# Low parts of the gate/up weight pairs made by ScalarE and an accumulating transfer instead of VectorE

## The chip, the core and the metric

The kernel runs on one core of a Trainium2 chip. The core has five engines that run side by side and meet only at semaphores: TensorE (PE, matrix products), VectorE (DVE), ScalarE (ACT), GpSimd (POOL) and SyncE (SP, which here only issues transfers). DMA engines move data between the chip's large memory (HBM) and the core's on-chip memory (SBUF). The metric is the device time of one execution in microseconds; lower is better.

## What is computed

A two-layer decoder trunk on 512 tokens of width 1024 in float32. Each layer has a mixer (pooling and gating in layer 0, dilated attention and retention in layer 1), an attention into 256 memory tokens, and a SwiGLU feed-forward part, each with its own norm and residual. The change touches the feed-forward part only:

```
D_FF = 2816
def swiglu(h, w_gate_up, w_down):
    gu = h @ w_gate_up
    g, u = gu[..., :D_FF], gu[..., D_FF:]
    return (jax.nn.silu(g) * u) @ w_down
...
h = h + swiglu(rmsnorm(h, ffn_norm[layer]), ffn_w_gate_up[layer], ffn_w_down[layer])
```

## The kernel before

**Three products for one.** Each float32 operand is split into a high part, the value rounded to TensorE's fast format fp32r, and a low part, the rest. A product is then hi x hi + hi x lo + lo x hi, three matmuls that add up in one PSUM bank. For the weights, ACT writes the high part (`w_hi` from `raw`, a copy that rounds) and DVE the low part (`w_lo = raw - w_hi`).

**Units and the ring.** Weights come from HBM in units of 128 x 1024 (512 KB). `raw`, `w_hi` and `w_lo` are rings of four units (RING = 4). SP loads them in order: before it loads a unit into a slot of `raw` it waits until the low part of the slot's last unit is made (semaphore `lo_ready`, which counts units). ACT may write `w_hi` in a slot when TensorE is done with what stood there.

**Gate/up in pairs.** The feed-forward part has 22 column tiles for gate and as many for up. The first four of each (PLAIN = 4) go through an ordinary loop. The other 18 steps of two tiles (PAIRS = 18, numbered q = 0 to 17, two units each, so that a pair fills half a ring) are computed with seven block products in the place of eight (a Strassen-like scheme). Products 1, 2, 4 and 7 read the weight pair's own parts (`w_hi`, `w_lo`), and products 5, 6 and 3 read sums of its blocks, which DVE makes into `s_f` (`first_sums`, `last_sum`) and ACT and DVE split into `s_hi` and `s_lo` (`sum_hi`, `sum_lo`). A product is 4 x 3 matmuls of 128 x 256.

**The order on TensorE** is `pair_steps()`: product 1 and 7 of pair q, product 3 of pair q-1, then products 6, 2, 4 and 5 of pair q, then product 1 of pair q+1, and so on. Product 1 of a pair is the first to read its `w_lo`, and the one that waits for it (`pe.wait_ge(lo_ready, pair_unit(layer, q) + 2)`).

**The order on ACT**, each q of the pair loop in `ffn`: copy product 6 of q out of PSUM (`copy_product`), `sum_hi(q+1)`, for even q two gate steps, `copy_product(q+1, 1)`, `pair_hi(q+2)` (the high parts of pair q+2, 128 x 2048), `copy_product(q+1, 7)`. TensorE's product 4 of pair q+1 waits for that last copy.

**The order on DVE**, each q: `last_sum(q+1)`, `pair_lo(q+1)` (the low parts of pair q+1), the quarters 11 and 21 of pair q, `sum_lo(q+1)`, quarter 22, `first_sums(q+2)`. `first_sums` of a pair overwrites one block of `raw` with a sum (semaphore `s3_ready`), and `pair_hi` waits for that.

POOL adds squares for the norms elsewhere. In the pair loop it has nothing to do, and it issues no transfer anywhere.

Of the kernel before, what the change touches and what calls it, by code (L numbers as in the profile page):

```python
# [35 lines left out]
F32 = mybir.dt.float32  # L36
F32R = mybir.dt.float32r
ACT = mybir.ActivationFunctionType
ALU = mybir.AluOpType
# [25 lines left out]
PAIRS = FT - PLAIN  # L65
# [11 lines left out]
F_DN, F_END = 2 * FT, 2 * FT + 2 * len(DOWN)  # L77
# [98 lines left out]
def program(nc, d):  # L176
    who, aux_at = aux_plan()

    with ExitStack() as ctx:
        def sem(name):  # L180
            return ctx.enter_context(nc.semaphore(name))
# [77 lines left out]
        raw = fixed("raw", [P, RING, UW])  # L259
        w_hi = fixed("w_hi", [P, RING, UW], F32R)  # L260
        w_lo = fixed("w_lo", [P, RING, UW], F32R)
# [88 lines left out]
        bhi_ready = sem("bhi_ready")  # L350
        blo_ready = sem("blo_ready")
        s3_ready = sem("s3_ready")
        s_ready = sem("s_ready")
        shi_ready = sem("shi_ready")
        slo_ready = sem("slo_ready")
# [118 lines left out]
        def pair_unit(layer, q):  # L474
            return F_UNIT[layer] + 2 * PLAIN + 2 * q

        def pair_cols(ring, layer, q):

            n = pair_unit(layer, q) % RING
            return ring[:, n:n + 2, :]  # L480

        def region_a(q):
            return accs[2 * (q % 2)][:, 0:S // 2]
# [170 lines left out]
        def _(act):  # L654
# [186 lines left out]
            def ffn(layer):  # L841
# [22 lines left out]
                def pair_hi(q):  # L864

                    n = pair_unit(layer, q)
                    act.wait_ge(raw_in[n % RING], 16 * (n // RING + 1))
                    act.wait_ge(s3_ready, PAIRS * layer + q + 1)
                    slot_free(act, n - RING)
                    slot_free(act, n + 1 - RING)  # L870
                    act.activation(pair_cols(w_hi, layer, q), pair_cols(raw, layer, q), ACT.Copy).then_inc(hi_ready, 2)  # L871

                def sum_hi(q):

# [332 lines left out]
        @block.gpsimd  # L1207
        def _(pool):
            pool.memset(warm_w[:, :], 0.0).then_inc(const_set, 1)
            pool.memset(mean_w[:, :], 1.0 / D).then_inc(const_set, 1)  # L1210
            pool.memset(mexp[:, :], -0.5).then_inc(const_set, 1)
            pool.memset(a_pad[:, :, 0:PAD], 0.0).then_inc(const_set, 1)
            pool.wait_ge(const_set, 4)

            def power(dst, src, n):
                pool.tensor_tensor(dst, src, mexp[:, 0:n], ALU.pow).then_inc(rstd_ready, 1)

            def norm_power(norm):

                pool.wait_ge(aux_free_v, freed_v(aux_at["mean", norm]))  # L1220
                power(rstd_tok[:, :], var_e[:, :], TT)

            def add_squares(norm, tiles=KT):
                for j in range(1, tiles):
                    n = (KT - 1) * (norm - 1) + j
                    pool.wait_ge(sq_ready, 8 * (norm - 1) + j + 1)
                    if j > 1:
                        pool.wait_ge(sq_added, n - 1)
                    pool.tensor_tensor(sqsum[:, :], sqsum[:, :], tmp[:, j % 2, :], ALU.add).then_inc(sq_added, 1)  # L1229

            pool.wait_ge(var_ready, 1)
            power(rstd_m[:, :], var_m[:, :], MT)
            pool.wait_ge(var_ready, 2)
            power(rstd_tok[:, :], var_e[:, :], TT)
            pool.wait_ge(c0_in, 16 * 5)

            pool.affine_select(out=ws_t[:, :, :], in_=ws_t[:, :, :], compare_op=ALU.is_ge, fill=0.0, base=0,
                               pattern=[[0, 4], [1, P]], channel_multiplier=-1).then_inc(ws_masked, 1)

            steps = 0  # L1240
            for g, win in enumerate(WINDOWS):
                pool.wait_ge(acc_drained, MIX_ACC[0] + A_A + g + 1)
                if g == 0:
                    pool.wait_ge(var_ready, 3)
                    power(rstd_v[:, :], var_v[:, :], TT)
                if g:

                    pool.wait_ge(win_ready, g)
                src, width = a_pad[:, g, :], 1
                buf = 0  # L1250
                while width < win:
                    last = 2 * width == win
                    if last and g >= 1:

                        pool.wait_ge(d_ready, g)
                    dst = wsum[:, 2 if last else buf, :]
                    lo = 2 * width - 1
                    ins = pool.tensor_tensor(dst[:, lo:PAD + S], src[:, lo:PAD + S],
                                             src[:, lo - width:PAD + S - width], ALU.add)
                    if last:  # L1260
                        ins.then_inc(win_ready, 1)
                    else:
                        ins.then_inc(win_step, 1)
                        steps += 1
                        pool.wait_ge(win_step, steps)
                    src, buf, width = dst, 1 - buf, 2 * width
            for layer in range(LAYERS):
                if layer:
                    add_squares(3)
                    norm_power(3)  # L1270

                    for r in range(16):
                        dst = rot_tile(r)
                        pool.wait_ge(rot_half, r + 1)
                        pool.tensor_tensor(dst, dst, tmp[:, 2 + r % 2, :], ALU.add).then_inc(rot_ready, 1)
                    for h in range(RET_H):
                        pool.wait_ge(rvar_ready, h + 1)
                        pool.tensor_tensor(rrstd[:, h, :], rvar[:, h, :], mexp[:, :], ALU.pow)\
                            .then_inc(rrstd_ready, 1)
                for norm in (3 * layer + 1, 3 * layer + 2):  # L1280
                    add_squares(norm)
                    norm_power(norm)
            add_squares(6, KT - 2)
            for e in range(2):
                pool.wait_ge(aux_free_v, freed_v(aux_at["mean", 6, e]))
                power(rstd_tok[:, 2 * e:2 * e + 2], var_e[:, 2 * e:2 * e + 2], 2)
# [3 lines left out]
        def _(dve):  # L1290
# [8 lines left out]
            def split(n, i=None):  # L1299
                if n >= UNITS:  # L1300
                    return
                s = n % RING
                dve.wait_ge(hi_ready, lin(n + 1, i, RING))
                dve.tensor_tensor(w_lo[:, s, :], raw[:, s, :], w_hi[:, s, :].bitcast(F32), ALU.subtract)\  # L1304
                    .then_inc(lo_ready, 1)
# [322 lines left out]
            def ffn(layer):  # L1628
# [50 lines left out]
                def last_sum(q, i):  # L1679

                    n, sums = pair_unit(layer, q), s_f[q % 2]
                    if q >= 2:
                        dve.wait_ge(product_done, product_at(layer, q - 2, 3))
                    dve.wait_ge(dve_step, i)
                    dve.tensor_tensor(sums[:, 2, :], sums[:, 1, :], raw[:, n % RING, 512:1024], ALU.add).then_inc(s_ready, 1)

                def pair_lo(q):
                    dve.wait_ge(hi_ready, pair_unit(layer, q) + 2)
                    dve.tensor_tensor(pair_cols(w_lo, layer, q), pair_cols(raw, layer, q),  # L1689
                                      pair_cols(w_hi, layer, q).bitcast(F32), ALU.subtract).then_inc(lo_ready, 2)  # L1690
# [181 lines left out]
                for q in range(PAIRS):  # L1872
                    last = q == PAIRS - 1
                    if q and q % 2 == 0:
                        up_second(q - 1)
                    if last:
                        split(u0 + F_DN)
                        split(u0 + F_DN + 1)
                    else:
                        if q:  # L1880
                            last_sum(q + 1, i)
                        pair_lo(q + 1)
                    if q == 0:
                        b_lo_part(3)
                    if last:
                        quarter(q, 11)
                        quarter(q, 22)
                        act_lo_part(7)
                        quarter(q, 21)
                    else:  # L1890
                        quarter(q, 11)
                        quarter(q, 21)
                        sum_lo(q + 1)
                        quarter(q, 22)
                    if q + 2 < PAIRS:
                        i = first_sums(q + 2)
                    if q % 2:
                        up_first(q)
                        up_tile(q)
                    if q in (10, 12, 14):  # L1900
                        act_lo_part(4 + (q - 10) // 2)
                    if last:
                        act_lo_part(8)
# [1008 lines left out]
```

## Time and profile before

| | us |
|---|---|
| median of 3 runs (1385.01 to 1385.16) | 1385.08 |
| span of the profiled execution | 1383.4 |
| TensorE busy (99% of the span) | 1374.1 |
| VectorE busy (70%) | 961.5 |
| ScalarE busy (48%) | 663.8 |
| GpSimd busy (8%) | 114.9 |

The span runs from the first to the last instruction of one profiled execution on the core; the median of the times lies 1.7 us above it. Busy time of an engine counts its computing instructions; registers, semaphores and issued transfers are not counted. A wait is put down to the engine and line that ended it.

### The profile page before, as it was taken

What the parts mean: (1) busy time and instruction counts of PE and PEld (TensorE: products, weight loads), DVE (VectorE), ACT (ScalarE), POOL (GpSimd) and SP (SyncE); (2) the same over time, 40 slices, a digit from 0 to 9 for tenths busy, and PEclk for the clock granted to TensorE, in tenths of its full rate; (3) what the DMA queues carried; (4) which work ended last, traced back from release to release, by engine and by line L of the source; (5) the groups of instructions that cost most, each with busy time, mean ns of one, the idle gap of its engine ahead of it and who ended that gap; (6) DMA issues with size and microseconds to landing.
All of it is one profiled execution on the core that took longest, in us unless ns stands there. A gap on an engine that the chain in (4) does not pass through costs nothing.

```text
span 1383.4 us, 21582 instructions
## 1 busy us (share of the span) xinstructions
PE 1374.1 (99%) x8404; PEld 1225.5 (89%) x8404; DVE 961.5 (70%) x1335; ACT 663.8 (48%) x984; POOL 114.9 (8%) x89
## 2 busy tenths in 40 slices
PE   9999999999999999999999999999999999999997
PEld 8988888889999998998887788988888999998897
DVE  6656556469878877774578755765549888888674
ACT  6633534355455553352756634543454545545341
POOL 0012200110000000110211211100020000000011
PEclk9999999999999999999999999999999999999999
DMA  9721320222323233325321212542132223233321
GB/s 345 268 91 61 107 92 31 91 92 77 122 92 122 93 107 107 120 95 167 97 87 46 82 41 77 185 150 77 46 107 79 105 98 116 93 122 98 116 92 62
DMA packets 42285, 147.22 MB, mean 106 GB/s; under 512 B 5072, under 2 KB 5584, under 8 KB 42192
## 3 DMA queue, kind: packets, MB, share of 16 engines
q1 hardware_dynamic: 38592, 136.79, 28.8%
q10 hardware_dynamic: 3600, 9.12, 1.9%
q8 instruction: 67, 1.10, 0.3%
q14 instruction: 26, 0.21, 0.1%
HBM read 143.80 MB, written 2.10 MB: 105 GB/s over the span
## 4 chain that ended last, share of the span: by engine, by line
PE 96%; DVE 2%; issue 1%; ACT 1%; DMA 0%; POOLq 0%; POOL 0%; ACTq 0%; DVEq 0%
PE acc L2173 17%; PE acc L2175 17%; PE acc L2174 17%; PE acc L2521 8%; PE acc L2522 7%; PE acc L2523 7%; PE acc L2221 3%; PE acc L2223 3%; PE acc L2222 3%; PE aux L2572 2%; PE aux L2571 2%; PE aux L2570 2%; PE aux L2523 1%; PE aux L2522 1%; PE aux L2521 1%
## 5 line engine op out<-in xcount | busy, mean ns | idle before, releaser
L1304 DVE TENSOR_TENSOR w_lo<-raw,w_hi 128x1024 fp32r<-128x1024 f32 x165 | 205.6, 1251 | 123.6 <-ACT w_hi L663 123.2
L663 ACT ACTIVATE w_hi<-raw 128x1024 fp32r<-128x1024 f32 x165 | 173.2, 1052 | 98.6 <-PE acc L2175 55.2
L1229 POOL TENSOR_TENSOR sqsum<-sqsum,tmp 128x512 f32<-128x512 f32 x40 | 60.0, 1501 | 960.3 <-ACT tmp L950 637.0
L2173 PE MATMUL acc<-u_hi,w_hi 128*128 128x512 f32 x352 | 138.7, 394 | 0.0
L2175 PE MATMUL acc<-u_hi,w_lo 128*128 128x512 f32 x352 | 137.2, 390 | 0.0
L2174 PE MATMUL acc<-u_lo,w_hi 128*128 128x512 f32 x352 | 137.1, 389 | 0.0
L2521 PE MATMUL acc<-b_hi,s_hi 128*128 128x256 f32 x432 | 122.4, 283 | 0.0
L2522 PE MATMUL acc<-b_lo,w_hi 128*128 128x256 f32 x432 | 122.3, 283 | 0.0
L2522 PE MATMUL acc<-b_lo,s_hi 128*128 128x256 f32 x432 | 122.2, 283 | 0.0
L2523 PE MATMUL acc<-b_hi,w_lo 128*128 128x256 f32 x432 | 122.2, 283 | 0.0
L2523 PE MATMUL acc<-b_hi,s_lo 128*128 128x256 f32 x432 | 122.2, 283 | 0.0
L2521 PE MATMUL acc<-b_hi,w_hi 128*128 128x256 f32 x432 | 122.2, 283 | 0.0
L2173 PE MATMUL acc<-y_hi,w_hi 128*128 128x512 f32 x256 | 100.1, 391 | 0.0
L2175 PE MATMUL acc<-y_hi,w_lo 128*128 128x512 f32 x256 | 99.7, 389 | 0.0
L2174 PE MATMUL acc<-y_lo,w_hi 128*128 128x512 f32 x256 | 99.6, 389 | 0.0
L2173 PE MATMUL acc<-act_hi,w_hi 128*128 128x512 f32 (+1 forms) x252 | 92.6, 367 | 0.0
L2174 PE MATMUL acc<-act_lo,w_hi 128*128 128x512 f32 (+1 forms) x252 | 92.2, 366 | 0.0
L2175 PE MATMUL acc<-act_hi,w_lo 128*128 128x512 f32 (+1 forms) x252 | 92.1, 365 | 0.0
L884 ACT ACTIVATE tmp<-acc 128x256 f32<-128x256 f32 x108 | 40.5, 375 | 96.4 <-PE acc L2523 96.4
L1689 DVE TENSOR_TENSOR w_lo<-raw,w_hi 128x2048 fp32r<-128x2048 f32 x36 | 82.2, 2284 | 2.2 <-ACT w_hi L871 2.2
L2521 PEld LDWEIGHTS acc<-b_hi,s_hi 128*128 128x128 f32 x432 | 82.9, 192 | 0.2
L2521 PEld LDWEIGHTS acc<-b_hi,w_hi 128*128 128x128 f32 x432 | 82.9, 192 | 0.1
(311 smaller groups left out, 3611.0 us busy)
## 6 DMA issues: line engine op xcount, KB each, us to landing
raw<-in_weights SPq DMA_DIRECT2D x253, 512.0 KB, 3.4
hT<-in_x_t ACTq DMA_DIRECT2D x4, 512.0 KB, 8.2
x_tok<-in_x ACTq DMA_DIRECT2D x4, 512.0 KB, 5.1
raw<-in_weights SPq DMA_DIRECT2D x5, 256.0 KB, 6.1
mem_tok<-in_mem ACTq DMA_DIRECT2D x2, 512.0 KB, 5.8
out_h<-out_f SPq DMA_DIRECT2D x2, 512.0 KB, 2.6
memT<-in_mem_t SPq DMA_DIRECT2D x3, 256.0 KB, 6.3
cs_d<-in_cs_d ACTq DMA_DIRECT2D x1, 512.0 KB, 4.3
```

What stands on the lines that cost most here:

```text
L663: act.activation(w_hi[:, s, :], raw[:, s, :], ACT.Copy).then_inc(hi_ready, 1)
L1229: pool.tensor_tensor(sqsum[:, :], sqsum[:, :], tmp[:, j % 2, :], ALU.add).then_inc(sq_added, 1)
L1304: dve.tensor_tensor(w_lo[:, s, :], raw[:, s, :], w_hi[:, s, :].bitcast(F32), ALU.subtract)\
L1689: dve.tensor_tensor(pair_cols(w_lo, layer, q), pair_cols(raw, layer, q), pair_cols(w_hi, layer, q).bitcast(F32), ALU.subtract).then_inc(lo ...
L2173: pe.matmul(out, w_h, x_h, start=first, stop=False)
L2174: pe.matmul(out, w_h, x_l, start=False, stop=False)
L2175: return pe.matmul(out, w_l, x_h, start=False, stop=last)
L2221: pe.matmul(out, x_h[:, k, tok], w_hi[:, s, w], start=(k == 0), stop=False)
L2222: pe.matmul(out, x_h[:, k, tok], w_lo[:, s, w], start=False, stop=False)
L2521: pe.matmul(out, hi[:, w], x_h, start=(k == 0 and m in (1, 2, 7)), stop=False, skip_group_check=True)
L2522: pe.matmul(out, hi[:, w], x_l, start=False, stop=False, skip_group_check=True)
L2523: ins = pe.matmul(out, lo[:, w], x_h, start=False, stop=(k == 3), skip_group_check=True)
```

## The change

For pairs q = 2 to 17 of both layers (32 pairs), DVE no longer makes the low parts. Instead

- ACT, right behind the high parts, writes `-round(raw)` into `w_lo` (a copy of 128 x 2048 with scale -1, counted by `neg_ready`);
- POOL waits for that and issues a transfer of `raw` into `w_lo` that adds (`accum_op=ALU.add`), 128 x 2048, 1 MB, SBUF to SBUF, so that `w_lo` holds `raw - w_hi`;
- POOL then waits for the earlier low parts (`lo_ready`), for the pair's last sum (`s_ready`, which also reads `raw`) and for the transfer (`low_in`), and adds 2 to `lo_ready`, on which both TensorE and SP wait.

Pairs 0 and 1 keep `pair_lo`. Of the last iteration, DVE waits until the last pair's count is in before it adds its own.

```
+        def nth(layer, q):
+            return (PAIRS // 2 - 1) * layer + q // 2
...
                     act.activation(pair_cols(w_hi, layer, q), pair_cols(raw, layer, q), ACT.Copy).then_inc(hi_ready, 2)
+                    if q >= 2:
+                        act.activation(pair_cols(w_lo, layer, q), pair_cols(raw, layer, q), ACT.Copy, scale=-1.0)\
+                            .then_inc(neg_ready, 1)
...
+            def low_parts(layer, q):
+                n = pair_unit(layer, q)
+                pool.wait_ge(neg_ready, (PAIRS - 2) * layer + q - 1)
+                pool.dma_start(pair_cols(w_lo, layer, q).bitcast(F32), pair_cols(raw, layer, q), accum_op=ALU.add)\
+                    .then_inc(low_in[q % 2], 16)
+                pool.wait_ge(lo_ready, n)
+                pool.wait_ge(s_ready, PAIRS * layer + q + 1)
+                pool.wait_ge(low_in[q % 2], 16 * nth(layer, q))
+                pool.sem_inc(lo_ready, 2)
...
                 for norm in (3 * layer + 1, 3 * layer + 2):
                     add_squares(norm)
                     norm_power(norm)
+                for q in range(2, PAIRS):
+                    low_parts(layer, q)
...
                     if last:
+                        dve.wait_ge(lo_ready, u0 + F_DN)
                         split(u0 + F_DN)
                         split(u0 + F_DN + 1)
+                    elif q:
+                        last_sum(q + 1, i)
                     else:
-                        if q:
-                            last_sum(q + 1, i)
-                        pair_lo(q + 1)
+                        pair_lo(1)
```

On ACT, in the pair loop of layer 0, the rows from the first copy ahead of `pair_hi(2)` to `sum_hi(3)` before:

```order
L884 ACTIVATE tmp<-acc 128x256
L871 ACTIVATE w_hi<-raw 128x2048
L884 ACTIVATE tmp<-acc 128x256
L896 ACTIVATE tmp<-acc 128x256
L884 ACTIVATE tmp<-acc 128x256
L876 ACTIVATE s_hi_64<-s_f_60 128x1536
```

and now:

```order
L893 ACTIVATE tmp<-acc 128x256
L877 ACTIVATE w_hi<-raw 128x2048
L879 ACTIVATE w_lo<-raw 128x2048
L893 ACTIVATE tmp<-acc 128x256
L905 ACTIVATE tmp<-acc 128x256
L893 ACTIVATE tmp<-acc 128x256
L885 ACTIVATE s_hi_64<-s_f_60 128x1536
```

The negated write stands behind the high parts and ahead of the copy of product 7, of a gate step and of the next sum's high parts.

On DVE, one iteration of the pair loop in layer 0, from `last_sum(3)` on, before:

```order
L1685 TENSOR_TENSOR s_f_61<-s_f_61,raw 128x512
L1689 TENSOR_TENSOR w_lo<-raw,w_hi 128x2048
L1709 TENSOR_TENSOR tmp<-aux,tmp 128x256
L1709 TENSOR_TENSOR tmp<-acc,tmp 128x256
L1694 TENSOR_TENSOR s_lo_63<-s_f_61,s_hi_65 128x1536
```

and now:

```order
L1707 TENSOR_TENSOR s_f_61<-s_f_61,raw 128x512
L1731 TENSOR_TENSOR tmp<-aux,tmp 128x256
L1731 TENSOR_TENSOR tmp<-acc,tmp 128x256
L1716 TENSOR_TENSOR s_lo_63<-s_f_61,s_hi_65 128x1536
```

The 128 x 2048 subtraction is gone; nothing else changes its place.

On POOL, from layer 0's last norm ahead of its feed-forward part to the norm behind it, now (before, the row with DMA is not there):

```order
L1225 TENSOR_TENSOR rstd_tok<-var_e,mexp 128x4
L1244 DMA w_lo<-raw 128x2048 x16
L1238 TENSOR_TENSOR sqsum<-sqsum,tmp 128x512 x7
```

The 16 transfers stand between the two norms, on a queue that held no transfer.

## Rows read from the trace of the kernel before

**Rows 1.** Page, busy time of each engine (share of the span) xinstructions.

```profile
PE 1374.1 (99%) x8404; PEld 1225.5 (89%) x8404; DVE 961.5 (70%) x1335; ACT 663.8 (48%) x984; POOL 114.9 (8%) x89
```

**Rows 2.** Page, shares of the chain that ended last, by engine.

```profile
PE 96%; DVE 2%; issue 1%; ACT 1%; DMA 0%; POOLq 0%; POOL 0%; ACTq 0%; DVEq 0%
```

**Rows 3.** Stretches of both pair loops: busy us of each engine, clock, DMA.

```profile
core 0: us, PE busy (x) PEld busy (x) DVE busy (x) ACT busy (x) POOL busy (x), PEclk, DMA share, GB/s
325.00:495.00 170.00, 170.00 (x1404) 169.34 (x1403) 143.97 (x183) 85.68 (x113) 0.00 (x0) 1.00 0.30 106
1080.00:1250.00 170.00, 170.00 (x1418) 169.90 (x1418) 139.78 (x180) 87.10 (x117) 0.00 (x0) 1.00 0.30 109
```

**Rows 4.** Timeline of PE at first matmuls of products: start us, us, what.

```profile
407.53 0.28 PE L2521 MATMUL acc<-b_hi,w_hi 128*128 128x256 f32 x1
407.65 0.28 PE L2522 MATMUL acc<-b_lo,w_hi 128*128 128x256 f32 x1
...
414.73 0.28 PE L2521 MATMUL acc<-b_hi,w_hi 128*128 128x256 f32 x1
...
417.61 0.28 PE L2521 MATMUL acc<-b_hi,w_hi 128*128 128x256 f32 x1
```

**Rows 5.** Timeline of ACT in the same pair: start us, us, what, idle before.

```profile
409.17 0.38 ACT L884 ACTIVATE tmp<-acc 128x256 f32<-128x256 f32 x1 [4.00 <-PE acc L2523]
410.07 1.91 ACT L871 ACTIVATE w_hi<-raw 128x2048 fp32r<-128x2048 f32 x1 [0.52 <-DVE raw L1674]
411.89 0.37 ACT L884 ACTIVATE tmp<-acc 128x256 f32<-128x256 f32 x1
413.49 0.38 ACT L884 ACTIVATE tmp<-acc 128x256 f32<-128x256 f32 x1 [1.23 <-PE acc L2523]
413.77 1.48 ACT L876 ACTIVATE s_hi<-s_f 128x1536 fp32r<-128x1536 f32 x1
```

**Rows 6.** Timeline of DVE in the same pair.

```profile
412.83 0.68 DVE L1685 TENSOR_TENSOR s_f<-s_f,raw 128x512 f32<-128x512 f32 x1
413.43 2.29 DVE L1689 TENSOR_TENSOR w_lo<-raw,w_hi 128x2048 fp32r<-128x2048 f32 x1
```

**Rows 7.** Groups by line and form: xcount, busy us, mean ns, idle before.

```profile
L1689 DVE TENSOR_TENSOR w_lo<-raw,w_hi 128x2048 fp32r<-128x2048 f32 x36 | 82.2, 2284 | 2.2 <-ACT w_hi L871 2.2
L871 ACT ACTIVATE w_hi<-raw 128x2048 fp32r<-128x2048 f32 x36 | 69.0, 1916 | 15.3 <-DVE raw L1674 8.3 <-issue 6.7
```

**Rows 8.** Timeline of SP's queue: the two loads (1 MB) of one pair issued.

```profile
405.04 0.92 SPq L638 DMA_DIRECT2D raw<-in_weights  x2
```

**Rows 9.** Transfers from 404.5 to 410.5: GB/s in 40 slices of 0.15 us, queue.

```profile
GB/s 0 0 0 0 0 0 0 0 0 0 273 137 27 82 246 328 410 410 382 437 437 410 410 410 437 437 410 437 437 246 164 27 0 0 0 0 0 0 0 0
q1 hardware_dynamic: 288, 1.05, 50.7%
raw<-in_weights SPq DMA_DIRECT2D x2, 512.0 KB, 3.7
```

**Rows 10.** Timeline in layer 0: ACT's high parts of pair 2, PE's product 1 of pair 2.

```profile
340.99 1.92 ACT L871 ACTIVATE w_hi<-raw 128x2048 fp32r<-128x2048 f32 x1 [0.42 <-issue]
...
347.05 0.28 PE L2521 MATMUL acc<-b_hi,w_hi 128*128 128x256 f32 x1
```

**Rows 11.** The same high parts of pair 2 in layer 1, on ACT.

```profile
1085.31 1.92 ACT L871 ACTIVATE w_hi<-raw 128x2048 fp32r<-128x2048 f32 x1 [0.42 <-issue]
```

**Rows 12.** A group of POOL instructions by line and form, columns as in rows 7.

```profile
L1229 POOL TENSOR_TENSOR sqsum<-sqsum,tmp 128x512 f32<-128x512 f32 x40 | 60.0, 1501 | 960.3 <-ACT tmp L950 637.0 <-ACT tmp L672 322.7
```

**Rows 13.** Stretches at the program's end, columns as in rows 3.

```profile
1368.00:1372.00 4.00, 4.00 (x36) 4.00 (x35) 2.65 (x7) 0.42 (x1) 0.00 (x0) 1.00 0.02 6
1372.00:1376.00 4.00, 3.36 (x29) 3.15 (x28) 1.33 (x4) 0.08 (x1) 0.00 (x0) 1.00 0.65 262
1376.00:1383.00 7.00, 1.01 (x6) 0.71 (x6) 1.42 (x4) 1.89 (x3) 0.70 (x1) 0.68 0.40 150
```

More of the change, by code:

```diff
@@ L352, in program @@
         s3_ready = sem("s3_ready")
+        neg_ready = sem("neg_ready")
+        low_in = [sem(f"low_in{e}") for e in range(2)]
         s_ready = sem("s_ready")
```

## The prediction

> **What bounds the kernel.** I read the busy shares first: TensorE has 99% of the span, VectorE 70%, ScalarE 48% [rows 1]. The chain that ended last agrees: 96% of it is TensorE [rows 2]. Then I looked at the two stretches that the change touches. In both pair loops TensorE is busy for all of 170 us at full clock [rows 3]. So it waits for nobody there, and work taken from DVE gives no time back by itself. What can change the time is a wait of TensorE that is not there now. The only thing of this change that TensorE reads is a pair's low part, at the start of product 1. The question is whether the new way delivers it in time.
>
> **The clock of a pair.** Call t(q) the start of product 1 of pair q. In one pair of the steady state it is 407.53, and the next pair's is 417.61 [rows 4]: 10.08 us, seven products of 12 matmuls at 0.12 us, 1.44 us each. Before, the low parts that are needed at 417.61 come from DVE's subtraction at 413.43, 2.29 us long, so at 415.72 [rows 6]: 1.9 us of slack.
>
> **What goes.** 32 subtractions of 2284 ns [rows 7], 73 us of DVE. They lay beside TensorE's work with 1.9 us of slack, so their going is worth nothing. DVE's other work in the loop waits for products.
>
> **What comes on ACT.** 32 negated writes of 128 x 2048. The trace has no such write with a scale, but the same shape and copy takes 1916 ns [rows 7], and behind one the next instruction starts 1.82 us after it began (410.07 to 411.89) [rows 5]. In all 61 us on an engine busy for about half of the stretch. Queued behind it is the copy of product 7, for which product 4 waits. It would start at 411.89 + 1.92 = 413.81 and end at 414.18, and product 4 starts at 414.73 [rows 4, 5]. That just holds, so the delayed copies cost nothing; the next sum's high parts come at most about 1 us later, and the product that reads them is seven microseconds off.
>
> **What comes on the path.** The low parts are now ready after high parts, negated write, and transfer. Let D be the time from the end of the negated write to TensorE's release: POOL wakes, writes the transfer's descriptors, the data move, the semaphore comes back, POOL adds to `lo_ready`. Without any wait, the high parts start 2.54 us after t [rows 4, 5], so there are 10.08 - 2.54 - 1.82 - 1.92 = 3.8 us for D.
>
> Once TensorE waits, a tighter loop closes. On ACT `pair_hi(q+2)` is queued behind the copy of product 1 of pair q+1, which itself needs t(q+1). That copy starts 409.17 - 407.53 = 1.64 us after t [rows 4, 5]; an instruction behind such a copy starts 0.28 us later (413.49 to 413.77) [rows 5]; the high parts take 1.82 and the negated write 1.92. So t(q+2) = t(q+1) + 5.66 + D, against 10.08 now. The wait is D - 4.42 **for each pair**, and the next pair cannot start its chain earlier while TensorE stands. It is not shared between two pairs, although the ring has room for two.
>
> **The size of D.** No row shows an accumulating transfer, nor one issued by POOL. The nearest is a plain 1 MB: the two loads of a pair. They are issued from 405.04, for 0.92 us [rows 8], so the second near 405.5, and each lands 3.7 us after its issue, 409.2 in all. The bytes have stopped there too [rows 9]. That is 4.2 us. The 16 DMA engines were busy for 50.7% of 6 us [rows 9], 3.0 us for one MB. To add, a DMA engine has to read the old `w_lo` as well as `raw`, twice the bytes read, so I take another 3.0. For the three semaphore hops and POOL's own writing of descriptors I take 0.8: more than the 0.46 that SP takes for each of its two issues [rows 8], less than the 1.5 us of a small POOL instruction [rows 12]. D = 4.2 + 3.0 + 0.8 = 8.0 us.
>
> Its bounds: 4.5 if the second read is free, which needs reads to be no limit at all; 6.0 if it is half hidden; 11.7 if the two reads and the write go one after another and POOL needs 1.5 (4.2 + 3.0 + 3.0 + 1.5). A gain is excluded, since TensorE waits nowhere in the stretch. Twice the bytes to read is the nearest, as the plain loads already run at 410 to 437 GB/s [rows 9], a level that looks like a ceiling.
>
> By the Trainium skill (DMA: Bandwidth & Descriptors, section on the anatomy of one DMA on the gpsimd path) such a transfer costs about 2.0 us fixed and its bytes at 436 GB/s, 4.4 us for 1 MB; the trace's 4.2 agrees. Its page Collectives: The Full Stack (section on the bandwidth ceiling) says that an adding transfer is not slowed by the add but by its two source reads, and runs at half the rate of a copy. By these two pages D would be 2.0 + 2 x 2.4 = 6.8 us, an estimate, and the change would cost 80 us instead of what follows. No row here shows either of them for an adding transfer.
>
> **The sum.** In each layer pairs 3 to 17 wait D - 4.42 = 3.58 us, 15 x 3.58 = 53.7. Pair 2 has a chain of its own: its high parts start at 340.99, behind ACT's gate step, the negated write would end at 344.73, and product 1 starts at 347.05 [rows 10]. Its wait is D - 2.32 = 5.68. Layer 1 has the same place at 1085.31 [rows 11]. So (53.7 + 5.7) x 2 = 118.8 us, or 32 D - 137 in general. Span 1383.4 + 118.8 = 1502.2, and 1.7 us lie around the span: **1504 us**.
>
> **Costed at nothing.** SP now issues the loads of pair q+2 near t(q), 2 us later than before. They land after 4.2 us, and their first sum is needed 10 us after t(q). The adding transfer starts 5.7 us after t, when the load is through, so the two do not share DMA engines. If that cover fails, a transfer gains up to 3.0 us. DVE's wait for `lo_ready` in the last iteration ends before t(17), ahead of what it computes there. POOL's next norm comes long after its last transfer.
>
> **The rivals.**
> *No wait, no change* (4%): D is 3.8 or less, and 1385 stands. It needs a 1 MB adding transfer faster than the plain one's 4.2. TensorE's saturation holds in this case too, so faster is no more than 1%: it would need a wait that DVE ends, and the pair loops have none.
> *Cheap second read* (14%): reads and adds overlap and D lies between 4.5 and 6.2. At 5.5 the sum gives 32 x 5.5 - 137 = 39, 1424 us. For it: both sides are SBUF and HBM is not involved. Against it: the same DMA engines, already full with one read.
> *The clock falls too* (16%): TensorE would stand 3.6 us in every 13.7. The trace shows full clock while it is busy for 3.36 of 4 us, and a mean of 0.68, so partly its lower level of 1.2 GHz, when it was busy for 1.0 of 7 us [rows 13]. The new loop lies between. At half clock the one product between t and ACT's copy takes 1.44 us longer, and only that one stands on the loop: 32 x 1.44 = 46, so 1550 us. The skill (TensorE: Matmul & The Clock Gate, section on oscillation) tells of a kernel whose waits put the clock down again in every tile. That would be this case.
> *A slow maker of descriptors or a slow adder* (15%): POOL makes 128 rows of descriptors with reads and writes, and a POOL add of only 128 x 512 already takes 1.5 us [rows 12]. At D = 12 the sum is 247, 1632 us; from D = 11 on this case holds.
> *Forecast* (50%): D from 6.2 to 11, 1446 to 1600 us, likeliest 1504.
>
> **How the numbers follow.** A measurement of this kernel can tell about 0.2%, 2.8 us, from no change; that needs D below 4.4. Slower has 95%, same 4%, faster 1%. The range runs from 1430 (D = 5.7) to 1620 (D = 11.6); it leaves out no change, half of the cheap read and two thirds of the slow adder, some 2 in 10.
>
> **What would show it.** Right: TensorE's matmul at product 1 waits about 3.6 us once in every pair from 2 to 17, 32 times, longer at pair 2, and nowhere else new. A pair's period is 13.7. ACT shows a second 1.9 us instruction behind each `w_hi`, then 8 us to the next product 1. DVE busy falls by 73 us, ACT rises by 61. If waits stand at every second pair only, the loop over the copy is wrong and the one over `first_sums` holds. If periods are right but D is 6 or 12, only its size was wrong. If the copy of product 7 makes product 4 wait, the slack of 0.5 us was misread. A PEclk below 1.00 in the pair loops is the clock rival.

## The result and the profile after

The changed kernel takes 1519.9 us (median of 4 runs, 1516.9 to 1523.6) against 1385.1 us: the ratio is 1.097, with a 95% interval of 1.096 to 1.099. Forecast were 1504 us and a range of 1430 to 1620. The span of the profiled execution grew from 1383.4 to 1516.8 us, by 133.4.

The page of the kernel after: first the busy time of each engine, then two rows of forty slices of the span (busy tenths of TensorE, and its granted clock), then the adding transfers as a queue (packets, MB, share of 16 engines) and as a group of issues (KB, us from issue to landing).

```profile
PE 1416.4 (93%) x8404; PEld 1261.1 (83%) x8404; DVE 893.0 (59%) x1303; ACT 719.8 (47%) x1016; POOL 143.0 (9%) x121
...
PE   9999999997778879999999999999998878879998
...
PEclk9999999998898999999999999999999999999999
...
q0 software_dynamic: 4608, 33.56, 11.0%
...
w_lo<-raw POOLq DMA_DIRECT2D x32, 1024.0 KB, 7.0
```

Against [rows 1], TensorE issues the same 8404 matmuls but is busy for only 93% of a longer span. The missing time sits in two places of the forty slices, the two pair loops. The clock's digit falls below nine in the first of them; in the second the mean is 0.93, as a row further down shows. The groups by instruction name the work: DVE loses the 32 subtractions of 2284 ns [rows 7], 73 us, and ACT gets 32 writes of 1902 ns, 61 us. (The busy figures of the whole engine move by 68.5 and 56.0 only, because neighbouring records overlap by some 0.1 us and the page counts that time once.)

TensorE's waits, the two rows on the pair loops (us in all, times, longest; the other six, elsewhere, are of 1.2 us or less, once each):

```profile
PE acc L2544 <- POOLq L1249: 89.2, 32, 4.7
PE acc L2544 <- ACT tmp L893: 1.4, 2, 0.7
```

L2544 is the first matmul form of products 1, 7, 4 (L2521 in [rows 4]) and L1249 is POOL's `sem_inc(lo_ready, 2)`. So TensorE now waits for the low parts once in each of the 32 pairs, a wait that did not exist before, and twice for a copy of ACT, in all 1.4 us. One turn of the loop, on ACT, POOL and TensorE (start us, us, what, and in brackets the idle time before it and what ended it):

```profile
411.88 0.58 PE L2544 MATMUL acc<-b_hi,w_hi 128*128 128x256 f32 x1 [3.64 <-POOLq L1249]
...
426.33 0.38 PE L2544 MATMUL acc<-b_hi,w_hi 128*128 128x256 f32 x1 [2.79 <-POOLq L1249]
...
439.49 0.58 PE L2544 MATMUL acc<-b_hi,w_hi 128*128 128x256 f32 x1 [2.83 <-POOLq L1249]
```

```profile
414.85 0.39 ACT L893 ACTIVATE tmp<-acc 128x256 f32<-128x256 f32 x1 [9.13 <-PE acc L2546]
415.13 1.90 ACT L877 ACTIVATE w_hi<-raw 128x2048 fp32r<-128x2048 f32 x1
416.93 1.90 ACT L879 ACTIVATE w_lo<-raw 128x2048 fp32r<-128x2048 f32 x1
418.73 0.38 ACT L893 ACTIVATE tmp<-acc 128x256 f32<-128x256 f32 x1
```

```profile
402.53 0.88 POOL L1244 DMA_DIRECT2D w_lo<-raw  x1 [13.47 <-ACT w_lo L879]
...
419.20 0.87 POOL L1244 DMA_DIRECT2D w_lo<-raw  x1 [15.80 <-DVE s_f L1707]
```

Read it as a circle. Product 1 starts at 411.88; ACT can copy it at 414.85, and that copy holds up the next pair's high parts (415.13) and negated write (416.93, through at 418.83). POOL issues the transfer at 419.20, and TensorE gets product 1 of the next pair at 426.33, 7.5 us after the negated write's end. From 426.33 to 439.49 are 13.16 us, where [rows 4] show 10.08.

Three stretches and the granted clock in them: inside the wait that ends at 411.88, just behind it, and each pair loop as a whole.

```profile
core 0: us, PE busy (x) PEld busy (x) DVE busy (x) ACT busy (x) POOL busy (x), PEclk, DMA share, GB/s
408.00:411.00 3.00, 0.24 (x3) 0.04 (x1) 3.00 (x6) 0.00 (x0) 0.00 (x0) 1.00 0.25 49
412.00:415.00 3.00, 3.00 (x15) 3.00 (x16) 0.01 (x1) 0.15 (x1) 0.00 (x0) 0.51 0.66 232
325.00:535.00 210.00, 172.20 (x1258) 168.68 (x1257) 98.36 (x151) 101.58 (x115) 12.47 (x14) 0.90 0.54 143
1130.00:1340.00 210.00, 174.83 (x1279) 169.35 (x1278) 108.70 (x160) 105.70 (x118) 11.34 (x13) 0.93 0.54 143
```

After a wait of 3.64 us the clock is at 0.51, the 1.2 GHz level, and 3 us hold 15 matmuls where [rows 4] have one each 0.12 us, 25. This is why ACT's copy above comes 2.97 us behind t, not 1.64.

### The profile page after: what moved, and what is told of

It is laid out like the page before. It is cut to its first block and busy times, and to the rows that moved or that the text cites. A ratio compares the mean times of both kernels' runs of the same rounds, so it can differ in the third digit from the quotient of the medians.

```text
span 1516.8 us, 21648 instructions
## 1 busy us (share of the span) xinstructions
PE 1416.4 (93%) x8404; PEld 1261.1 (83%) x8404; DVE 893.0 (59%) x1303; ACT 719.8 (47%) x1016; POOL 143.0 (9%) x121
## 5 line engine op out<-in xcount | busy, mean ns | idle before, releaser
L2544 PE MATMUL acc<-b_hi,w_hi 128*128 128x256 f32 x432 | 141.1, 327 | 90.6 <-POOLq L1249 89.2
L2544 PEld LDWEIGHTS acc<-b_hi,w_hi 128*128 128x128 f32 x432 | 97.5, 226 | 97.6 <-POOLq L1249 95.7
L2545 PE MATMUL acc<-b_lo,w_hi 128*128 128x256 f32 x432 | 136.7, 317 | 0.0
L2546 PE MATMUL acc<-b_hi,w_lo 128*128 128x256 f32 x432 | 136.5, 316 | 0.0
L2544 PE MATMUL acc<-b_hi,s_hi 128*128 128x256 f32 x432 | 123.8, 287 | 0.0
L2545 PEld LDWEIGHTS acc<-b_lo,w_hi 128*128 128x128 f32 x432 | 98.1, 227 | 0.1
L2546 PEld LDWEIGHTS acc<-b_hi,w_lo 128*128 128x128 f32 x432 | 98.0, 227 | 0.0
```

The costliest lines, as they stand in the source:

```text
L2544: pe.matmul(out, hi[:, w], x_h, start=(k == 0 and m in (1, 2, 7)), stop=False, skip_group_check=True)
L2545: pe.matmul(out, hi[:, w], x_l, start=False, stop=False, skip_group_check=True)
L2546: ins = pe.matmul(out, lo[:, w], x_h, start=False, stop=(k == 3), skip_group_check=True)
```

## The experiments

All times are medians; each kernel is compared with the kernel before in the same series. "After" is the changed kernel. The kernel before took 1385.2 us in each series of experiments; after was timed in the series of the result, against 1385.1 us. D is, as in the prediction, the time from the end of the negated write to TensorE's product 1.

**1. The negated writes alone.** POOL's transfers go, DVE subtracts as before, behind the negated write (the subtraction overwrites it).

```
-                for q in range(2, PAIRS):
-                    low_parts(layer, q)
...
-                    elif q:
-                        last_sum(q + 1, i)
                     else:
-                        pair_lo(1)
+                        if q:
+                            last_sum(q + 1, i)
+                            dve.wait_ge(neg_ready, (PAIRS - 2) * layer + q)
+                        pair_lo(q + 1)
```

> ACT's negated write stays where it is, but POOL issues no transfer: DVE waits for the negated write and makes the low parts itself by its subtraction, as before. Computes the same as before. Theory (the transfer's time is the whole cost, ACT's extra 1.9 us hides): negated write ends 6.3 us after t(q), subtraction 2.3 us more, 8.7 of 10.08, so no wait of TensorE at product 1: 1385 to 1387 us. Rival (ACT's queue is the cost: the copies of products 7 and 6 behind the negated write make TensorE wait): 0.5 us or more at product 4 in most pairs, 1400 us and above.

Measured: 1388.8 us, ratio 1.0026 (1.0015 to 1.0037). So ACT's 61 us of extra work cost 3.6 us, small but not nothing: above the 1385 to 1387 of the theory, far below the 1400 of the rival. Where: TensorE's wait at product 4 of pair 1, once in each layer, and ACT, then PE, in a pair of the steady state.

```profile
PE acc L2542 <- ACT tmp L893: 1.4, 2, 0.7
...
346.88 0.39 PE L2542 MATMUL acc<-b_hi,w_hi 128*128 128x256 f32 x1 [0.70 <-ACT tmp L893]
```

```profile
405.39 1.90 ACT L879 ACTIVATE w_lo<-raw 128x2048 fp32r<-128x2048 f32 x1
407.19 0.36 ACT L893 ACTIVATE tmp<-acc 128x256 f32<-128x256 f32 x1
...
407.66 0.34 PE L2542 MATMUL acc<-b_hi,w_hi 128*128 128x256 f32 x1
```

The copy of product 7 runs from 407.19 to 407.55 and product 4 starts at 407.66, 0.11 us behind. The slack of 0.55 us that the prediction read is used up: periods are 10.11 to 10.13 us here (one is 10.41) and 10.08 before. Pair 1 takes 11.19, 0.96 us more, in each layer. From product 1 of pair 0 to that of pair 17 the two loops are 1.9 and 1.6 us longer than before, together 3.5. The rest of the 133 us must come from the transfer and what its waits bring about.

**2. A plain transfer.** The same 1 MB from `raw` to `w_lo`, without the add; the low parts are then the raw weights, so the result is wrong.

```
-                pool.dma_start(pair_cols(w_lo, layer, q).bitcast(F32), pair_cols(raw, layer, q), accum_op=ALU.add)\
+                pool.dma_start(pair_cols(w_lo, layer, q).bitcast(F32), pair_cols(raw, layer, q))\
```

> The transfer that POOL issues copies raw into w_lo in the place of adding it (the low parts of pairs 2 to 17 are wrong: they hold the raw weights). Same bytes written, half the bytes read. Theory (the second read is what makes the data phase twice as long): bytes move in 2.6 us in the place of 4.9, D falls from 7.45 to about 5.1, 32 x 5.1 - 137 = 26 us over before, about 1411 us, clock mostly full. Rival (what POOL's queue and descriptor writing cost dominates, whatever is moved): D stays at 7 or more, 1490 to 1520 us.

Measured: 1415.8 us, ratio 1.0217 (1.0200 to 1.0234). Without the add 104 of the 135 us are gone. TensorE's wait, the transfer's median landing time, and the transfer's queue in a window of 10 us around one of them:

```profile
PE acc L2544 <- POOLq L1249: 18.5, 31, 1.8
...
w_lo<-raw POOLq DMA_DIRECT2D x32, 1024.0 KB, 4.6
...
q0 software_dynamic: 144, 1.05, 27.3%
```

D is 4.9 to 5.1 us in most pairs, which is the sum of what the prediction made of the plain parts: 4.2 for 1 MB and 0.8 for the hops. At 5.0 the sum 32 D - 137 gives 23 us of the 30.7 measured. The trace accounts for the rest: some pairs have a D of 5.2 to 5.8, so with each pair's own D the sum is 26; TensorE waits for the copy of product 7 at pair 1 (1.9), and the negated write ends later behind t than 5.66 (3.4 in all). That makes 31.5, where the span grew by 30.0.

**3. An adding transfer of half the size.** Only the pair's first unit (512 KB) is added; the second unit keeps the negated high parts, so half of each pair's low parts are wrong.

```
-                pool.dma_start(pair_cols(w_lo, layer, q).bitcast(F32), pair_cols(raw, layer, q), accum_op=ALU.add)\
+                pool.dma_start(w_lo[:, n % RING, :].bitcast(F32), raw[:, n % RING, :], accum_op=ALU.add)\
```

> The adding transfer covers only the first unit of each pair, 512 KB in the place of 1 MB (left out: the addition for the second unit, whose low parts stay minus the rounded weights). Same bytes read in all as the plain transfer of 1 MB. Theory: data phase about 2.5 us, D about 5.1, the same time as the plain 1 MB, about 1411 us. Rival (adding has a fixed cost of its own, not one by bytes): D near 7, time 1480 and above.

Measured: 1417.5 us, ratio 1.0234 (1.0217 to 1.0251). The same three views:

```profile
PE acc L2544 <- POOLq L1249: 22.0, 32, 1.9
...
w_lo<-raw POOLq DMA_DIRECT2D x32, 512.0 KB, 4.5
...
q0 software_dynamic: 144, 0.52, 27.6%
```

Half a megabyte with the add costs what a whole one costs without: 27.6% against 27.3% of 10 us on the DMA engines, and D 5.0 to 5.1 in most pairs. So the price of adding goes by the bytes and is no fixed cost. If an adding transfer reads both operands, both kernels read 1 MB, and the bytes read explain the equal times. But an adder that takes bytes in at half the rate of a copy would give the same two numbers: no run here tells the two apart. Experiments 2 and 3 came out 5 and 6.5 us above the 1411 expected; seven late transfers (below) are 5.0 us of it here.

**4. The other order on ACT.** The copy of product 1 of pair q+1 goes between the high parts and the negated write of pair q+2, where after has it ahead of both.

```
                     act.activation(pair_cols(w_hi, layer, q), pair_cols(raw, layer, q), ACT.Copy).then_inc(hi_ready, 2)
                     if q >= 2:
+                        copy_product(q - 1, 1)
...
-                    if not last:
-                        copy_product(q + 1, 1)
```

> Only ACT's order changes: the copy of product 1 of pair q+1 stands between the high parts and the negated write of pair q+2, not ahead of both. Computes the same. Theory (ACT's loop over that copy closes at every pair, period 5.66 + D): the high parts then no longer wait for product 1, the loop is the one over first_sums and two pairs, 10.08 + 6.5 + 7.45 = 24.1 us for two pairs, 12.0 each in the place of 13.1; waits of about 63 us in all and less loss of clock: 1465 to 1480 us. Rival (another loop sets the period, such as POOL's own queue or the loads): no change, 1515 to 1525 us.

Measured: 1478.8 us, ratio 1.0669 (1.0652 to 1.0687), 41 us less than after with the same transfers. ACT:

```profile
1183.52 1.91 ACT L877 ACTIVATE w_hi<-raw 128x2048 fp32r<-128x2048 f32 x1 [0.70 <-DVE raw L1696]
1185.34 0.37 ACT L894 ACTIVATE tmp<-acc 128x256 f32<-128x256 f32 x1
1185.60 1.90 ACT L880 ACTIVATE w_lo<-raw 128x2048 fp32r<-128x2048 f32 x1
```

DVE ahead of them, quarter 21 of the pair that starts at 1170.81, and the sum that releases the high parts:

```profile
1179.74 0.42 DVE L1731 TENSOR_TENSOR tmp<-acc,tmp 128x256 f32<-128x256 f32 x1 [1.01 <-PE acc L2546]
...
1182.68 0.69 DVE L1696 TENSOR_TENSOR raw<-raw 128x512 f32<-128x512 f32 x1
```

TensorE at product 1 of three pairs:

```profile
1170.81 0.39 PE L2544 MATMUL acc<-b_hi,w_hi 128*128 128x256 f32 x1 [1.70 <-POOLq L1249]
...
1183.09 0.39 PE L2544 MATMUL acc<-b_hi,w_hi 128*128 128x256 f32 x1 [1.96 <-POOLq L1249]
...
1194.88 0.39 PE L2544 MATMUL acc<-b_hi,w_hi 128*128 128x256 f32 x1 [1.45 <-POOLq L1249]
```

The high parts no longer wait for the copy of product 1: what releases them is DVE's `first_sums` (L1696). The copy stands right behind them without idle time, so it does not wait for TensorE either. The loop over that copy is open here, and the expectation's other one closes: product 1 at 1170.81, DVE's quarter of that pair, `first_sums`, the high parts from 1183.52, the negated write through at 1187.50, the transfer, and product 1 at 1194.88. That is 24.07 us for two pairs, against 24.1 expected. A wait stands in every pair all the same, since the pairs between run a loop of their own; so the prediction's sign for this loop, a wait at every second pair only, would have missed it.

In 25 of the 32 pairs the copy stands right behind the high parts; in the other 7 it does wait for TensorE, by 0.1 to 2.8 us, and most of these are pairs with the low clock or behind a late transfer. The three pairs shown are among the shortest: the mean period is 12.9 and 12.5 us in the two loops, against 14.4 and 13.8 in the changed kernel.

**5. TensorE kept busy while it waits.** Ahead of the wait at product 1, 18 matmuls into a PSUM bank that is free there, results unused.

```
+                    if m == 1 and q >= 2:
+                        for _ in range(18):
+                            pe.matmul(auxs[2][:, 0:S // 2], b_hi[:, 0, 0, 0:P], b_hi[:, 0, 0, :], start=True, stop=True,
+                                      skip_group_check=True)
```

> 18 idle matmuls of 128 x 256 (2.2 us, into a PSUM bank that nobody reads) stand ahead of TensorE's wait at product 1 of pairs 2 to 17; otherwise the changed kernel. The rest is computed as before. Theory (the part of the loss above the bare waits is the clock, which falls because TensorE stands, and the waits are set by the chain on ACT, POOL and DMA and not by TensorE's own time): the fill fits into the 3 us of waiting, the clock stays full, periods are 13.1 us and the time is 1385 + 101 + 2 to 3 for ACT's copies and about 10 for slow transfers, 1495 to 1502 us. Rival (the longer periods come from the transfers and not from the clock): same as the changed kernel, 1517 to 1524 us. Rival (TensorE's own time stands on the loop): 32 x 2.2 = 70 us slower.

Measured: 1501.7 us, ratio 1.0846 (1.0828 to 1.0864), 18.2 us less than after, though it computes more. The page's clock row, one filled wait, and 2 us behind it:

```profile
PEclk9999999999999999999999999999999999999999
```

```profile
403.94 2.32 PE L2525 MATMUL aux<-b_hi 128*128 128x256 f32 x18
406.99 0.39 PE L2548 MATMUL acc<-b_hi,w_hi 128*128 128x256 f32 x1 [0.74 <-POOLq L1249]
```

```profile
407.00:408.00 1.00, 1.00 (x8) 1.00 (x9) 0.86 (x2) 0.00 (x0) 0.00 (x0) 1.00 0.00 0
408.00:409.00 1.00, 1.00 (x10) 1.00 (x10) 0.00 (x0) 0.27 (x1) 0.00 (x0) 1.00 0.84 279
```

The clock stays at 1.00 behind this wait, and half of the 30 periods are 13.1 to 13.3 us. Nearly all the others are longer by a late transfer (below). But the clock does not hold everywhere: its records show about 14 us at the 1.2 GHz level in the two loops, in four stretches, three of them behind a late transfer; the changed kernel has 85 us. In the four pairs after these stretches the period is 13.8 us, and TensorE, with its unused matmuls, reached the wait only when the low parts were there. So what the clock cost is about 18 us. The changed kernel's own trace agrees: the negated write ends 5.72 us behind t where product 1 runs at full clock and up to 7.1 where it does not, in sum 18 us over the 30 pairs. The loop itself is untouched, since idle matmuls bring no low part sooner.

**6. The pair's transfer in two halves.** Each unit has an adding transfer of its own; TensorE waits for the first at product 1 and for the second at product 7.

```
+                for e in range(2):
+                    s = (n + e) % RING
+                    pool.dma_start(w_lo[:, s, :].bitcast(F32), raw[:, s, :], accum_op=ALU.add)\
+                        .then_inc((low_in, low_b)[e][q % 2], 16)
...
+                    if m in (1, 7):
+                        pe.wait_ge(lo_ready, pair_unit(layer, q) + (1 if m == 1 else 2))
```

> The adding transfer of a pair is cut into two of 512 KB, one for each unit, and TensorE waits for the first at product 1 and for the second at product 7. Computes the same. Theory (D is 2.5 us fixed and 5 us for 1 MB, and DMA engines work through one transfer after the other): the first unit is there 5.05 us after the negated write, the second about 7.6; period 11.2 to 11.5 us, about 1425 to 1440 us. Rival (the two transfers share the DMA engines packet by packet and land together near 7.5, or POOL's second issue holds up the first): period 13 us, 1500 us and above.

Measured: 1444.2 us, ratio 1.0436 (1.0418 to 1.0455), 76 us less than after. TensorE's waits (L1252 counts the first unit, L1254 the second), POOL's issue, and products 1 (420.27) and 7 (411.07, 423.07):

```profile
PE acc L2549 <- POOLq L1254: 33.0, 29, 2.3
PE acc L2549 <- POOLq L1252: 9.1, 11, 2.2
```

```profile
415.52 1.78 POOL L1247 DMA_DIRECT2D w_lo<-raw  x2 [10.19 <-ACT w_lo L880]
```

```profile
411.07 0.39 PE L2549 MATMUL acc<-b_hi,w_hi 128*128 128x256 f32 x1 [0.58 <-POOLq L1254]
...
420.27 0.39 PE L2549 MATMUL acc<-b_hi,w_hi 128*128 128x256 f32 x1 [0.30 <-POOLq L1252]
423.07 0.38 PE L2549 MATMUL acc<-b_hi,w_hi 128*128 128x256 f32 x1 [1.11 <-POOLq L1254]
```

Product 1 now starts 4.75 us after POOL began to issue, not 7.1, and product 7 after 7.55. The second half binds: it comes as late as the whole did, plus 0.4 us, but is needed a product later. In 11 of the 32 pairs product 1 still waits for its half; in the others TensorE, held up at product 7 of the pair before, comes later by itself. The period from product 1 to product 1 goes between 11.4 and 12.0 us, with two of 14.0 and 14.2; the mean is 11.7, above the 11.2 to 11.5 expected, and the time lies 4 us above the expected range. The shorter waits leave the clock at 0.996 over the span. Of the forms run that keep the transfer and compute the right result this is the fastest, and it is still 59 us slower than the kernel before. None could be faster than that kernel by what is taken from DVE, since TensorE was busy for 170 of 170 us at full clock [rows 3].

## Where the prediction was right and where not

**The bound and the place: right.** TensorE had nothing to gain [rows 3], and the new wait is at product 1 in pairs 2 to 17, 32 times (4.2 us idle at pair 2 of layer 0, some 2.8 in the steady pairs; a matmul's record is 0.28 us long where one starts each 0.12, so the idle time shown falls a little short of the wait).

**The loop per pair: right.** The period at full clock, without a late transfer, is 13.13 to 13.2 us, and 5.66 + 7.45 = 13.11. With D at 5.05 (experiment 3) it is 10.7 to 10.8, and 5.66 + 5.05 = 10.71. Experiment 4 takes the copy out of the high parts' way, and another loop with a shorter period takes over.

**D: the add was sized too high.** D was put at 4.2 + 3.0 + 0.8 = 8.0 us and measures 7.45 (7.38 to 7.64 in pairs without a late transfer). The two outer terms were right as a sum: the plain transfer of experiment 2 has D = 5.0. Their split was not: 4.6 from issue to landing and some 0.5 on the two sides. The add costs 7.45 - 5.0 = 2.45 us, not 3.0, and 0.33 of that is POOL's longer issue (0.87 us in place of 0.54). The 3.0 came from 50.7% of 6 us [rows 9], which is two loads out of HBM; a copy within SBUF holds the DMA engines for only 27.3% of 10 us, 2.7, and the adding one for 51.8%, 2.45 more. That took 17.6 us off the sum: 32 x 7.45 - 137 is 101. The prediction's lower bounds do not fit its own terms: with the second read free, 4.2 + 0.8 is 5.0, not 4.5.

The two pages of the Trainium skill gave D = 6.8. Their rule that an adding transfer is held back by its two source reads (Collectives: The Full Stack, section on the bandwidth ceiling) agrees with experiments 2 and 3, equal time for equal bytes read, though they do not show that the reads are the reason. For the plain 1 MB, DMA: Bandwidth & Descriptors made 4.4 us of the fixed cost and the bytes, and the trace has 4.6 to landing. What their sum lacked is the semaphore path on either side of the transfer. By 6.8 the bare waits would be 81 us; they are 101.

**A term was missing: late transfers, 9.8 us.** Beside the data, the trace has fetches of instructions on the DMA engines. From the start of POOL's issue to product 1, 25 of the 32 transfers take 7.08 to 7.31 us. The other 7 take 7.57 to 9.35, 9.8 us more in sum. Here are GB/s in forty slices of 0.25 us, and the queues, for a normal one (from 419.20) and for the latest (from 402.50):

```profile
GB/s 0 0 0 0 0 262 262 0 524 0 229 295 0 524 0 197 328 0 524 0 229 295 0 524 0 0 0 0 0 0 0 0 82 164 115 328 426 442 328 459
...
q0 software_dynamic: 144, 1.05, 51.8%
```

```profile
GB/s 0 0 0 0 0 131 393 0 492 33 197 328 0 426 98 66 459 0 459 66 131 393 0 459 66 0 0 0 66 0 0 0 0 0 0 0 0 0 0 0
...
q0 software_dynamic: 144, 1.05, 52.2%
q8 instruction: 1, 0.02, 0.6%
```

Both transfers have started all their data packets within some 5 us of the first one, and the second one's window has an instruction fetch, the lone slice at 409.5. The single packets show where the delay sits. Each transfer ends with 16 packets of 4 bytes, as many as there are DMA engines. In the late one 15 of them stand 6.4 to 6.6 us behind the issue, as in the normal one, and the last stands at 8.11, where the fetch (7.16 to 8.12) ends. It is the same in all 7: the fifteenth by 6.63, the sixteenth at 6.8 to 8.2, where those of the 25 others are all there by 6.8. So 15 of 16 parts of the transfer are through in time, and the whole is held up by one.

All 7 late transfers have a fetch in their window and none of the 25 others has. Experiment 3 shows 7 and 25 again, experiment 5 shows 10 and 18 among the transfers that TensorE waited for, with no overlap but at the edge of experiment 3 (4.67 to 6.23 with a fetch, 4.66 to 4.88 without). In experiment 2 they overlap (issue to landing 4.6 to 5.0 with a fetch, 4.4 to 4.8 without). No run took the fetches away, so that they are the cause is argued from these traces and not tested by itself.

**The clock: the rival was half true.** The forecast took none of it and the clock rival 46 us; it cost 18 us by experiment 5 and by the negated writes' delay in the trace. The rival's mechanism is as it was told, one product at half clock between t and ACT's copy (14.45 us from 411.88 to 426.33). But it does not happen in each pair: the mean clock in the loops is 0.90 and 0.93. What the Trainium skill tells of waits that put the clock down again in every tile (TensorE: Matmul & The Clock Gate, section on oscillation) is borne out in part only.

**"The delayed copies cost nothing": wrong, by little.** Product 4 does wait for the copy of product 7: some 3.5 us in experiment 1, and two waits worth 1.9 us in after, where TensorE's other wait covers the steady pairs. The slack of 0.55 us was read from the copy's end to the matmul's start, and 0.11 of it is the handover itself. At pair 1 ACT was later than in the pair from which the slack was read.

**The loads: right.** In the first of the two bandwidth rows the adding transfer ends at 425.2 and the next pair's loads begin at 427.2, 0.9 us after product 1. They do not share the DMA engines, and in none of the 32 transfers does a load's packet start between POOL's issue and product 1.

**The sum again**, with what was measured: 101.2 (D) + 9.8 (late transfers) + 1.9 (copy of product 7) = 112.9; of the 20.5 left of 133.4, 18 are the clock, and 1.8 are 30 pairs in which ACT's step from t to the negated write's end takes 5.72 us where the prediction read 5.66 in a pair without a wait; 0.7 stay open. Against the prediction's 118.8: D 17.6 less, terms that it had at nothing 32.2 more. The time came out within 16 us because these errors have opposite signs, and that part is luck.

## What to carry to other kernels

Before moving work to an idle engine, see who waits for the busy one: 73 us off VectorE brought nothing that any trace shows, for it was ready 1.9 us ahead of a TensorE that never stood. When a hop is added on a path with little slack, follow the path once round: if the producer's queue holds something that needs the consumer's last step (here the copy of product 1), the whole latency counts in each turn, and a ring with room for two pairs did not share it between them (more room was not run). What shortens a turn then counts 32 times: a faster hop (104 us for the transfer without the add, which computes something else), handing over in halves (76 us), and the order in that queue (41 us for one moved copy). When one loop is opened, look for the next one: in experiment 4 it was the one over `first_sums`.

## What the runs showed of the hardware

- An adding transfer of 1 MB within SBUF took 7.0 us from issue to landing, a plain one 4.6, and an adding one of 512 KB 4.5. POOL held 0.87 us for the issue, in place of 0.54 for a plain one.
- The 7 of 32 transfers with an instruction fetch beside them completed 0.4 to 2.2 us late, by the last of 16 completion packets alone; cause not isolated.
- With a wait of TensorE of 1.3 to 4.7 us in each pair, its clock fell to the 1.2 GHz level behind some of them, not all (85 us at that level in the two loops). With 18 unused matmuls ahead of each wait it was 14 us, and the kernel 18 us faster.
